# Layer 1's FFN down projection with the activations stationary, and three steps moved ahead of their neighbours

## The reference

```python
f = _rmsnorm(h, g_ffn_pre)
ffn_out = (jax.nn.silu(f @ ffn_w_gate) * (f @ ffn_w_up)) @ ffn_w_down   # 2816 -> 1024
return h + _rmsnorm(ffn_out, g_ffn_post)                                # mean over the 1024 features
...
return h[:, BLOCK:, :]                                                  # after layer 1: the 256 real tokens
```

## Time and profile before

| | us |
|---|---|
| median of 3 runs | 989.2 (989.0 to 989.77) |
| the profiled execution, as timed | 990.38 |
| its span, first to last instruction | 988.6 |
| TensorE busy | 971.9 (98%) |
| VectorE, ScalarE, GpSimd busy | 591.5, 518.3, 84.3 |
| mean granted clock of TensorE | 0.995 of full speed |
| read from HBM | 154.45 MB, 157 GB/s over the span |

### The profile page before, as it was taken

The page is one execution under the profiler, slowest core; times in us unless marked ns, Lnnn a source line. Parts: engine busy times, 40 slices in busy tenths (PEclk is TensorE's granted clock), DMA queues, the critical chain, the costliest instruction groups (busy, mean ns, idle before and its releaser), DMA issues.

```text
span 988.6 us, 19698 instructions
## 1 busy us (share of the span) xinstructions
PE 971.9 (98%) x7726; PEld 924.6 (94%) x7726; DVE 591.5 (60%) x904; ACT 518.3 (52%) x832; POOL 84.3 (9%) x78
## 2 busy tenths in 40 slices
PE   8999999999999999999999999999999999999998
PEld 6999888899999999999979998888999899999996
DVE  7566565367957655554466665643678666666443
ACT  5543744475466544444455447444855665545542
POOL 1000000000031222200000000000000322211010
PEclk9999999999999999999999999999999999999998
DMA  6875434346462555555545654344464556655551
GB/s 179 282 231 158 127 105 128 113 126 164 154 213 84 181 178 177 179 167 176 155 128 171 192 170 124 93 128 129 134 185 152 170 156 186 196 184 173 195 185 43
DMA packets 170060, 157.51 MB, mean 159 GB/s; under 512 B 9603, under 2 KB 168558, under 8 KB 169614
## 3 DMA queue, kind: packets, MB, share of 16 engines
q1 hardware_dynamic: 168878, 153.24, 50.3%
q10 hardware_dynamic: 928, 3.33, 1.0%
q0 software_dynamic: 192, 0.07, 0.0%
HBM read 154.45 MB, written 1.05 MB: 157 GB/s over the span
## 4 chain that ended last, share of the span: by engine, by line
PE 91%; DVE 4%; ACT 2%; DMA 1%; issue 1%; ACTq 0%; DVEq 0%; SPq 0%
PE banks L645 26%; PE banks L647 25%; PE banks L646 25%; PE banks L695 2%; PE banks L680 2%; PE banks L676 1%; PE banks L677 1%; PE banks L885 1%; DVE lo L1413 1%; PE banks L883 1%; ACT hi L1066 1%; PE banks L625 1%; DVE sub L1441 1%; DMA raw<-in_ffn_w_up 1%; DMA raw<-in_w_out 1%
## 5 line engine op out<-in xcount | busy, mean ns | idle before, releaser
L645 PE MATMUL banks<-xh,hi 128*128 128x272 f32 (+1 forms) x1584 | 457.2, 289 | 0.2
L1413 DVE TENSOR_TENSOR lo<-raw,hi 128x1024 fp32r<-128x1024 f32 (+1 forms) x290 | 349.5, 1208 | 176.4 <-ACT hi L1066 175.6
L647 PE MATMUL banks<-xh,lo 128*128 128x272 f32 (+1 forms) x1584 | 452.9, 286 | 0.0
L646 PE MATMUL banks<-xl,hi 128*128 128x272 f32 (+1 forms) x1584 | 451.8, 285 | 0.0
L1066 ACT ACTIVATE hi<-raw 128x1024 fp32r<-128x1024 f32 (+1 forms) x290 | 302.0, 1042 | 108.1 <-PE banks L647 59.8
L645 PEld LDWEIGHTS banks<-xh,hi 128*128 128x128 f32 x1584 | 298.5, 188 | 6.6 <-issue 4.7
L647 PEld LDWEIGHTS banks<-xh,lo 128*128 128x128 f32 x1584 | 298.6, 188 | 0.0
L646 PEld LDWEIGHTS banks<-xl,hi 128*128 128x128 f32 x1584 | 298.2, 188 | 0.0
L647 PE MATMUL banks<-ah,lo 128*128 128x272 f32 (+1 forms) x352 | 100.8, 286 | 0.0
L645 PE MATMUL banks<-ah,hi 128*128 128x272 f32 (+1 forms) x352 | 100.4, 285 | 0.0
L646 PE MATMUL banks<-al,hi 128*128 128x272 f32 (+1 forms) x352 | 100.3, 285 | 0.0
(11 more groups left out here) (260 smaller groups left out, 1123.9 us busy)
## 6 DMA issues: line engine op xcount, KB each, us to landing
raw<-in_w_in SPq DMA_DIRECT2D x54, 1024.0 KB, 5.2
raw<-in_ffn_w_gate SPq DMA_DIRECT2D x22, 1024.0 KB, 5.3
raw<-in_ffn_w_up SPq DMA_DIRECT2D x22, 1024.0 KB, 5.3
raw<-in_ffn_w_down SPq DMA_DIRECT2D x16, 1024.0 KB, 5.1
raw<-in_w_out SPq DMA_DIRECT2D x8, 1024.0 KB, 5.2
raw<-in_w_in SPq DMA_DIRECT2D x12, 512.0 KB, 4.2
raw<-in_w_branch SPq DMA_DIRECT2D x12, 512.0 KB, 5.5
raw<-in_ffn_w_down SPq DMA_DIRECT2D x8, 768.0 KB, 4.3
```

Source lines behind the costliest of these rows:

```text
L645: mm(dst, wh, mh, start=start, stop=False)
L646: mm(dst, wh, ml, start=False, stop=False)
L647: return mm(dst, wl, mh, start=False, stop=stop)
L1413: tt(lo[g % 2][:, 0:k, f], raw[g % 2][:, 0:k, f], hi[g % 2][:, 0:k, f].bitcast(F32), ALU.subtract).then_inc(lo_ready, 2 if g in G_MIX else 1)
```

## The change

Layer 1's down projection is written anew (`down_rows`); layer 0's stays. The stationary side is now a block of activations, [128 features x 128 tokens], and the moving side is 512 columns of the weights, so the result comes out as rows of tokens: four tiles, two halves of the columns by two blocks of 128 tokens, each filling a PSUM bank. The weights come in 11 groups of 1 MB: four slabs by 512 columns, ten times, and one group (number 5) of two slabs by all 1024 columns. SyncE's loads move runs of 2 KB (4 KB in group 5) instead of 1 KB. Ahead of them SyncE loads the gain, one row of 1024 numbers, into all 128 partitions (`gain`, 512 KB). A half is now half the buffer in the order of the slabs, so the first half of each of the first two groups waits for both halves of the group two before.

The norm is done by rows: ScalarE squares a tile with the sum along the row as a by-product, and takes Ln and Exp of a [128 x 1] column; VectorE multiplies the tile by the gain, then by that column, and adds the transposed `hT`, which lies in PSUM. The transposes of `hT` as it is after the mixer stand before the last group (token block 0) and behind it (block 1). The last group does all of token block 0 first. In gate and up the last pass of ScalarE's and VectorE's loop is written out behind the loop.

The three moved steps: `sb_scores` of heads 0 and 1 comes ahead of `sb_scores0` and waits for the two tiles that it reads; `take_out(0)` comes ahead of `ml_soft`; in the last `branch` step the low part of the weight half comes ahead of `rest_of_merged`. The first two lists and all steps are the same for both layers.

```diff
-           ("sb_scores0",), ("sb_scores", 0), ("sb_scores", 1), ("sb_soft0",), ...
+           ("sb_scores", 0), ("sb_scores0",), ("sb_scores", 1), ("sb_soft0",), ...
-    4: [("ml_soft",), ("take_out", 0)],
+    4: [("take_out", 0), ("ml_soft",)],
+def row_slot(j, s):
+    if j == FULL_ROW:
+        return FT - 2 + s // 2, s % 2
+    return 4 * (j % (FULL_ROW + 1)) + s, int(j > FULL_ROW)
@@ SyncE
+                    sp.wait_ge(merge_step[l], KT)
+                    sp.dma_start(gain, norm_ffn_post[l:l + 1, :].broadcast_to((P, D))).then_inc(gain_loaded, 16)
+                    for j in range(NROWS):
+                        g = G_ROWS + j
+                        k, half = row_slot(j, 0)
+                        sp.wait_ge(hi_ready, 2 * (g - 1))
+                        sp.wait_ge(lo_ready, 2 * (g - 1))
+                        if j == FULL_ROW:
+                            sp.dma_start(by_rows(raw[g % 2], 2), wd[:, k:, :]).then_inc(raw_loaded[g % 2], 16)
+                        else:
+                            sp.dma_start(by_rows(raw[g % 2]), wd[:, k:k + 4, 512 * half:512 * half + 512]).then_inc(...)
@@ TensorE
+                for name in ("sbq", "sbk"):
+                    wait_taken(pe, group_tile(l, name) + i)
...
+                def quarter(j, s, b):
+                    k, half = row_slot(j, s)
+                    tok = slice(META + b * P, META + b * P + P)
+                    wh, wl = (by_rows(w[(G_ROWS + j) % 2])[:, s, :] for w in (hi, lo))
+                    first, stop = (0, FT - 1) if half == 0 else (FT - 2, FT - 3)
+                    dst = open_tile(t + 2 * half + b) if k == first else bank_of(t + 2 * half + b)
+                    mm(dst, ah[:, k, tok], wh, start=k == first, stop=False)
+                    mm(dst, ah[:, k, tok], wl, start=False, stop=False)
+                    last = mm(dst, al[:, k, tok], wh, start=False, stop=k == stop)
...
+                turn_h(0)
+                for b in range(2):
+                    for s in range(4):
+                        use_half(G_END - 1, s // 2)
+                        quarter(NROWS - 1, s, b)
+                turn_h(1)
@@ ScalarE
+                elif (g - 2 in SWAPPED or G_ROWS <= g < G_ROWS + 2) and c == 0:
                     act.wait_ge(half_used, n - 2)
...
+                for b in range(2):
+                    square(1, b)
+                    act.wait_ge(row_summed, 5 + b)
+                    fn(row_rstd[:, 2 + b:3 + b], row_ss[:, 2 + b:3 + b], ACT.Ln, scale=1.0 / D, bias=row_bias[:, b:b + 1])...
+                    act.wait_ge(row_rooted, 2 * b + 1)
+                    fn(row_rstd[:, b:b + 1], row_rstd[:, 2 + b:3 + b], ACT.Exp, scale=-0.5).then_inc(row_rooted, 1)
@@ VectorE
-                if m == KT - 1:
-                    rest_of_merged(l, m)
                 rest_of_half(at + REST_AHEAD)
-                if 0 < m < KT - 1:
-                    rest_of_merged(l, m - 1)
+                if m:
+                    rest_of_merged(l, m if m == KT - 1 else m - 1)
...
+                for b in range(2):
+                    scale(1, b)                      # otok = tile * gain, 128 x 512
+                    dve.wait_ge(row_scaled, 3 + b)
+                    dve.wait_ge(row_rooted, 2 * b + 2)
+                    for half in range(2):
+                        n, at = TILE_OUT + 2 * b + half, slice(512 * half, 512 * half + 512)
+                        wait_tile(dve, n)
+                        stt(otok[:, b, at], otok[:, b, at], row_rstd[:, b:b + 1], bank_of(n), ALU.mult, ALU.add)...
```

More of the change, by code:

```diff
@@ L272, in plan_tiles @@
     free(*RING, *RING, *RING[:DEPTH])
-    for _ in range(DEPTH):
+    for l in range(DEPTH):
         f = {}
@@ L301, in plan_tiles @@
         stage("down")
-        for n in range(KT // 2):
-            last_of(RING[2 * n % 4], 1, 2 * len(DOWN_K) - 2), last_of(RING[2 * n % 4 + 1])
-        stage("norm3"), free(NORM_BANK)
+        if l < DEPTH - 1:
+            for n in range(KT // 2):
+                last_of(RING[2 * n % 4], 1, 2 * len(DOWN_K) - 2), last_of(RING[2 * n % 4 + 1])
+            stage("norm3"), free(NORM_BANK)
+        else:
+            for n, bank in enumerate(RING):
+                signal.append(("rows", n + 1, 1))
+                put(bank)
         first.append(f)
@@ L488, in wait_tile @@
             per = SIGNAL[t + step][1] - n
-            eng.wait_ge(tile_done if kind == "tile" else half_used, n + i * per)
+            eng.wait_ge({"tile": tile_done, "half": half_used, "rows": rows_done}[kind], n + i * per)
         def bank_of(t):
@@ L996, in down, with turn_h, down_rows @@
                                 last.then_inc(half_used, 1)
+            def turn_h(b):
+                for half in range(2):
+                    n = TILE_OUT + 2 * b + half
+                    ps = open_tile(n)
+                    for c in range(4):
+                        wait_h(pe, DEPTH - 1, 1, 4 * half + c)
+                        last = nc.tensor.transpose(ps[:, c * P:c * P + P], hT[:, 4 * half + c, META + b * P:META + b * P + P], cut["ident"])
+                    close_tile(last, n)
+            def down_rows(l):
+                t = TILE[l]["down"]
+                def quarter(j, s, b):
[7 more added lines that the diff above has]
+                    last = mm(dst, al[:, k, tok], wh, start=False, stop=k == stop)
+                    if k == stop:
+                        last.then_inc(rows_done, 1)
+                    return last
+                for j in range(NROWS - 1):
+                    for c in range(2):
+                        use_half(G_ROWS + j, c)
+                        for s in (2 * c, 2 * c + 1):
+                            k, half = row_slot(j, s)
+                            if half == 0:
+                                pe.wait_ge(ah_ready[l], k + 1)
+                                pe.wait_ge(al_ready[l], k + 1)
+                            for b in range(2):
+                                last = quarter(j, s, b)
+                        last.then_inc(half_used, 1)
+                turn_h(0)
[4 more added lines that the diff above has]
+                turn_h(1)
             pe.wait_ge(misc_set, 2)
@@ L1390, in _ @@
                 exp_tables(l)
[L1391 to L1395, removed]
-                fn(otok[:, b, 512 * half:512 * half + 512], bank_of(TILE_OUT + n), ACT.Copy).then_inc(out_rows, 1)
+                if l < DEPTH - 1:
+                    down(l)
+                    root(l, 3, q0)
+                else:
+                    down_rows(l)
         @block.vector
@@ L1760, in gate_up, with pair @@
                     rest_of_prod(c, slice(c, c + 1), c + 1)
-                with dve.Fori(0, NGU // 2 - 1) as i:
+                def pair(i, n, *loop):
                     for c in range(2):
```

115 lines of the change are left out of this document (82 added, 33 removed).

## The result

The changed kernel takes **979.8 us** (median of 4, 978.57 to 980.76) where the kernel before, on the same chip, took 989.49 (989.0 to 990.21): 9.7 us less, ratio 0.990 (95% interval 0.9887 to 0.9912). A second session with five rounds gave 978.86 against 989.62, ratio 0.9889 (0.9872 to 0.9905). The forecast was 976.5, with 972.5 to 981.3 as its range.

What follows compares the result with a forecast made beforehand. TensorE was taken as the bound (98% busy, 91% of the chain of waits). Products 2.2, tail 6.8, scores 1.6, first take-out 1.5 and low part 0.6 sum to 12.7 us won: 976.5 us, range 972.5 to 981.3.

Steps and rivals of the forecast that it cites:

- I take 0.2258: Layer 1's down projection: 0.2258 us per 512-column product, extra paid per instruction, bounds 0.2133 and 0.2527; 2.2 us won.
- a share of the columns: Rival, down projection: the extra grows with the columns, 0.2367 us per product, 2.9 us more, 979.4; chance 0.20.
- The extra hides: Rival, down projection: the extra hides behind a wide product, 0.2133 us each, 3.3 us less, 973.2; chance 0.21.
- goes through twice: Rival, down projection: 512 four-byte columns stream at half rate, 0.427 us per product, 53 us more, 1029; chance 0.03.
- Transposes: Down projection: eight transposes of token block 0 now stand between the products and take 0.87 us.
- The supply: Down projection: weight loads and rounding keep up with TensorE and the gain's load delays nothing; cost nothing.
- The tail: Behind the last product: 5.4 us to the span's end instead of 12.2, 6.8 us won.
- Scores: Mixers of both layers: TensorE's 0.69 us wait for the last `sbk` tile goes; 0.8 us per layer, 1.6 in all.
- First take-out: Mixers: with the take-out moved ahead TensorE starts its next step earlier, 0.57 and 0.95 us by layer, 1.5 in all.
- Low part: Output projection: most of one wait turns into another at the last merged slab; 0.27 and 0.31 us won, 0.6 in all.
- The waits come back: Rival, three mixer places: ScalarE is no earlier, so TensorE, 3.7 us ahead, waits at the next bank; 980.2, chance 0.09.
- I take the same difference off the median: Span to time: profiled execution 990.38 lay 1.2 above the median 989.2; the same difference turns span 975.9 into 976.5.

Runs made afterwards that it cites:

- the last version: Changed kernel with the weight half's low part cut in two around the merged slab's, and `take_out(2)` ahead of logit 6; 980.0 us, ratio 0.9893 against before.
- floor: Changed kernel with down-projection products in some groups cut into four of 128, eight of 64 or two of 256 columns, others whole; 1073.26 us in one run.

## Why the prediction was right, and where it was not

*The products: the term that was mis-sized.* The step "I take 0.2258" for a product of 512 columns failed: it measured 0.2325. Over 263 distances that is 1.8 us, and the 2.2 us won between the first product and the last's end became 0.35. The bounds held (0.2133 and 0.2527). The reason given for 0.2258, that it lies near the middle of the bounds, was misread: the middle is 0.2330, almost what was measured. Of the two laws weighed, the extra per instruction was wrong. The rival "a share of the columns" (0.2367) came nearer, with the right mechanism in the main: the extra goes mostly with the columns. It was still 0.004 too high, since it took the share from 256 columns, where 2 ns more are lost. The argument against that share, that at 1.2 GHz nothing is on top, said nothing of the full clock: the changed stage shows 0.454 ns per four-byte column, less than the 0.835 that a column takes in those rows (0.2271 / 272), so a limit at that rate would not show there. The text had this as the rival's escape and gave it less weight than it deserved. "The extra hides" and "goes through twice" are both excluded by the rows.

*Transposes:* eight took 0.79 (964.46 to 965.25), 0.87 forecast. *The supply:* right, no idle time of TensorE; ScalarE's two long waits for loads of `ffn_w_down` (2.2 and 2.8 us) stayed covered, and VectorE never waited for the gain. In the middle of the stream stand two squares and not eight, at no cost either way.

*The tail:* 5.3 us from the last product's end, 5.4 forecast, 6.9 won instead of 6.8. The two small activations cost 0.29 and 0.20 instead of 0.31 each, and hid beside the product with the gain as said.

*Scores:* the wait went as forecast, but 0.56 was won in each layer instead of 0.8. The step "the scores of two heads ... now fill it" took the scores to last as long as before. They last 2.30 us (97.30 to 99.60) instead of 2.10 (99.30 to 101.40), since heads 0 and 1 no longer stand beside heads 2 and 3: each pair now takes 0.85 instead of 0.75. The first also starts 0.22 behind the product ahead of it, not 0.13. *First take-out:* 0.68 and 1.07, forecast 0.57 and 0.95; the 0.1 more comes one product behind the wait, where an idle TensorE had lost that as well (138.02 to 138.36, now 135.65 to 135.88). *Second take-out:* -0.17 and 0.36 at `take_out(2)`, no part of the forecast, follow ScalarE's issues and do not repeat. *Low part:* the mechanism was right, to the instruction and to its size: the product is 0.37 us late in layer 0, 0.38 forecast, and the net gain is 0.26 and 0.28, 0.27 and 0.31 forecast. (The 0.94 after which the rest "could" have started fits a start at 273.73, within the addition's overlap, and not the 273.81 named beside it.) *"The waits come back":* no, the moves alone gave 3.8 us. In a further step in the same direction 0.9 of 1.4 us did come back.

*From the span to the median.* The profiled span came out at 976.4, 0.5 from the forecast 975.9. The larger part of the 3.3 us between 976.5 and 979.8 is in the step "I take the same difference off the median". The profiled execution before lay 1.2 above its median; the one after lay 1.2 below its own. Its time was 2.2 above its span instead of 1.8, and this part is no scatter: it is in every execution with the rows. The kernel's executions differ by 2 us (978.57 to 980.76, spans 976.4 to 978.6). Most of such a difference arises before 24 us: there the changed kernel was 1.25 and 0.88 ahead of before in its two profiles, and the moves alone, the rows alone and the last version were 0.58, 0.50 and 0.79 behind, though all have the same work there. The first transpose starts at 6.54 in one and at 8.05 in another, where it waits for the tokens, and the stretch at half the clock falls elsewhere (17.8 to 21.2 us here, 19.8 to 23.2 before). What makes the first loads vary was not tried. Taking the difference as zero would have given 977.7 from the same sum.

The time fell within the range, but that the profiled span came out 0.5 from the forecast was luck. The terms of the change came to 10.7 us (1.12 scores, 1.75 first take-out, 0.54 low part, 0.35 products, 6.9 tail), against 12.7; 1.25 of the profiled difference was scatter in the launch and 0.2 at `take_out(2)`, and 0.36 outside the span was not thought of.

## What to carry to other kernels

To halve the count of matmuls by doubling their width wins only what each paid per instruction, and here that was little: two products of 256 columns took 0.2366 us, one of 512 took 0.2328, for the extra over the clock's rate went mostly with the columns. Before counting on it, cut a few products of a running kernel to other widths and read their distances. What pays at the end of a kernel is the chain behind the last product; and a difference of a microsecond between two profiled executions should first be located in time, since it may lie where the change does nothing. Such a place is found by reading the lead over the old kernel in the even stretches on both sides of each step, in several profiles: what the change did repeats to 0.03 us here, and the rest does not.

## What the runs showed of the hardware

- In products of 512 columns with a new stationary block each, four-byte (fp32r) operands took 0.454 ns per column at the full clock (0.2325 us), two-byte ones side by side 0.421 (0.2158), two-byte ones four bytes apart 0.442 (0.2265), with both sides of the product changed together. The Trainium skill, "SBUF — State Buffer", Door 1: The DMA port swizzle, says that SBUF has lines of 16 bytes, that a change of line costs something, and that two accesses to a line are enough for full bandwidth. Columns four bytes apart have four in a line, so by it they should cost nothing, and these rows do not agree: they cost 10 ns at the same type. Nor does it say anything of the 6 ns at equal spacing.
- With a load of a stationary block of 128 columns for each, an fp32r product takes at least 0.110 to 0.112 us at the full clock, for 64 columns as for 128.
- In the run `floor` the granted clock fell from 1.00 to 0.50 four times (924.8, 986.2, 996.4, 1023.7), each time in, or within 0.4 us behind, a stretch of products of 64 columns in which TensorE was never idle. In its stretches of 128 columns at the full clock (912.1 to 919.9, 970.5 to 981.1, 1009.1 to 1019.6) it did not fall.
- Four DMAs that ScalarE issues one behind the other (`rows`) kept it for 2.5 to 3.7 us in ten profiles, twice in each; in layer 1 TensorE waited for the take-out behind them in eight of the ten.
- The time outside the profiled span went from 1.75 to 1.84 us without the rows to 2.10 to 2.24 with them, whatever else was changed.
